# PSUM banks handed out by age, the scores of two heads in turn, and VectorE making the whole low half outside the experts

## The reference, cut to what matters

```python
logits = jnp.einsum('bhnid,bhnjd->bhnij', qb, kb) * SCALE
lo = jnp.where(ii[:, None] >= ii[None, :], lo + own_bias[None, :, None], NEG)
```

## Time and profile before

| | |
|---|---|
| median of three executions | 1948.52 us |
| profiled execution, its time | 1950.66 us |
| span of its instructions | 1948.9 us |
| TensorE matmul busy | 1788.9 us, 92% |
| VectorE busy | 1224.6 us, 63% |
| ScalarE busy | 968.1 us, 50% |
| GpSimd busy | 927.0 us, 48% |
| granted TensorE clock, mean | 0.944 |
| ScalarE's high half of a unit, mean | 1912 ns |
| HBM read | 336.76 MB |

### The profile page before, as it was taken

How to read it: one execution, slowest core, us unless ns; L and a number is a source line. 1 busy time by engine, 2 the same in 40 slices (tenths; PEclk the granted TensorE clock), 3 DMA queues, 4 the chain that set the end, 5 groups by cost and what they waited for, 6 DMA issues and landing times.

```text
span 1948.9 us, 30590 instructions
## 1 busy us (share of the span) xinstructions
PE 1788.9 (92%) x12222; PEld 1649.9 (85%) x12222; DVE 1224.6 (63%) x1841; ACT 968.1 (50%) x1406; POOL 927.0 (48%) x525
## 2 busy tenths in 40 slices
PE   6999999998899998989979999899878999999996
PEld 5988899987789998978879999778767878888875
DVE  4656554455554545866764444877767878787783
ACT  3455554345545533444435433444426767676762
POOL 5431566543136655312245446312243777786860
PEclk8999999999879999989989999889878999999996
DMA  6522345552224555322325445423325888888980
GB/s 242 195 89 101 127 172 178 195 195 87 87 88 165 181 176 205 131 86 84 112 87 173 173 176 172 164 88 108 109 87 194 316 309 323 299 324 308 340 307 24
DMA packets 50019, 339.95 MB, mean 174 GB/s; under 512 B 5511, under 2 KB 7775, under 8 KB 10031
## 3 DMA queue, kind: packets, MB, share of 16 engines
q1 hardware_dynamic: 47152, 328.79, 46.3%
q0 software_dynamic: 2720, 9.13, 1.5%
HBM read 336.76 MB, written 1.13 MB: 173 GB/s over the span
## 4 chain that ended last, share of the span: by engine, by line
PE 66%; DVE 17%; ACT 6%; issue 5%; POOL 3%; DMA 0%; DVEq 0%; SPq 0%; ACTq 0%; POOLq 0%
PE bank L408 11%; PE bank L410 11%; PE bank L409 11%; DVE CA L1657 5%; PE bank L786 4%; PE bank L787 4%; PE bank L788 4%; ACT wh L975 3%; DVE wl L1381 3%; POOL wl L1972 2%; PE bank L544 2%; PE bank L817 2%; PE bank L545 2%; PE bank L486 2%; PE bank L546 2%
## 5 line engine op out<-in xcount | busy, mean ns | idle before, releaser
L1972 POOL TENSOR_TENSOR wl<-stg,wh 128x512 fp32r<-128x512 f32 x311 | 784.6, 2529 | 856.1 <-ACT wh L975 855.4
L1381 DVE TENSOR_TENSOR wl<-stg,wh 128x1536 fp32r<-128x1536 f32 x311 | 592.6, 1911 | 343.0 <-ACT wh L975 342.6
L975 ACT ACTIVATE wh<-stg 128x2048 fp32r<-128x2048 f32 x311 | 594.2, 1912 | 231.2 <-PE bank L410 114.6
L408 PE MATMUL bank<-xh,wh 128*128 128x256 f32 (+1 forms) x1472 | 431.5, 293 | 10.0 <-POOL wl L1972 4.8
L410 PE MATMUL bank<-xh,wl 128*128 128x256 f32 (+1 forms) x1472 | 424.9, 289 | 0.0
L409 PE MATMUL bank<-xl,wh 128*128 128x256 f32 (+1 forms) x1472 | 424.4, 288 | 0.0
L408 PEld LDWEIGHTS bank<-xh,wh 128*128 128x128 f32 x1472 | 284.0, 193 | 13.9 <-issue 11.6
L409 PEld LDWEIGHTS bank<-xl,wh 128*128 128x128 f32 x1472 | 283.5, 193 | 0.7
L410 PEld LDWEIGHTS bank<-xh,wl 128*128 128x128 f32 x1472 | 283.9, 193 | 0.0
L544 PE MATMUL bank<-wh,xh 128*128 128x256 f32 x480 | 144.5, 301 | 33.9 <-DVE xl L1420 17.3
L786 PE MATMUL bank<-wh,GH 128*128 128x512 f32 (+3 forms) x400 | 148.0, 370 | 0.1
(11 more groups left out here) (256 smaller groups left out, 3211.5 us busy)
## 6 DMA issues: line engine op xcount, KB each, us to landing
stg<-in_w SPq DMA_DIRECT2D x311, 1024.0 KB, 4.8
BT<-bias_scratch POOLq DMA_DIRECT2D x3, 1024.0 KB, 11.4
BT<-bias_scratch POOLq DMA_DIRECT2D x1, 2048.0 KB, 12.2
BB<-bias_scratch POOLq DMA_DIRECT2D x2, 1024.0 KB, 8.2
res<-in_x SPq DMA_DIRECT2D x1, 1024.0 KB, 5.7
BB<-bias_scratch POOLq DMA_DIRECT2D x2, 512.0 KB, 8.6
out<-res SPq DMA_DIRECT2D x1, 1024.0 KB, 4.6
consts<-in_consts SPq DMA_DIRECT2D x1, 320.0 KB, 5.7
```

Source lines behind the costliest of these rows:

```text
L408: pe.matmul(out, wh, xh(kt), start=kt == 0, stop=False)
L975: act.activation(WH[u % NW][:, :], stg[u % NS][:, :], ACT.Copy).then_inc(*m.inc("w_high", u))
L1381: vec.tensor_tensor(WL[u % NW][:, 0:VW], stg[u % NS][:, 0:VW], WH[u % NW][:, 0:VW].bitcast(F32), ALU.subtract).then_inc(*m.inc("w_low_v", u))
L1972: pool.tensor_tensor(WL[u % NW][:, VW:], stg[u % NS][:, VW:], WH[u % NW][:, VW:].bitcast(F32), ALU.subtract).then_inc(*m.inc("w_low_g", u))
```

## The change

Three parts, all in one diff.

1. `bank` keeps a list `line` of the banks and gives the first one that is not held, moving it to the end; `let_go` moves banks that were held to the end of the list when they are released.
2. The jobs come in the order (head h, tt 0), (h+1, tt 0), (h, tt 1), (h+1, tt 1), and `scores` does nothing for odd i; for even i it issues the scores of jobs i and i+1, one matmul of each in turn. Their banks are taken together, for each group of segments one bank of each job.
3. For units under `MOE_UNIT` VectorE subtracts all 2048 columns and GpSimd none; the waits for GpSimd's part go for these units on TensorE and on the DMA queue. The experts keep the split at 1536.

```diff
-                    for hh in range(4 * hq, 4 * hq + 4):
+                    for h0, tt, hh in ((h0, tt, h0 + j) for h0 in (4 * hq, 4 * hq + 2) for tt in range(2) for j in range(2)):
...
-            turn, held, frees = [0], set(), [()] * 8
+            line, held, frees = list(range(8)), set(), [()] * 8
...
-                while turn[0] % 8 in held:
-                    turn[0] += 1
-                b = turn[0] % 8
-                turn[0] += 1
+                b = [i for i in line if i not in held][0]
+                line.remove(b)
+                line.append(b)
...
+            def let_go(*banks):
+                for b in banks:
+                    held.discard(b)
+                    line.remove(b)
+                    line.append(b)
...
-                w.wait_ge(*m.of("w_low_g", u))
+                if u >= MOE_UNIT:
+                    w.wait_ge(*m.of("w_low_g", u))
...
             def scores(l, i):
+                if i % 2:
+                    return
+                two = JOBS1[l][0][i:i + 2]
...
-                    b, old = bank(("score", l, i, s0), ("biased", (l, i, s0)))
-                    vacant(old)
+                    bs = [bank(("score", l, i + k, s0), ("biased", (l, i + k, s0))) for k in range(2)]
+                    for b, old in bs:
+                        vacant(old)
                     for n in range(s0, s1):
...
+                        for k in range(2):
+                            lhs, rhs = two[k]["segs"][n]
+                            ins = pe.matmul(PS[bs[k][0]][:, (n - s0) * wd:(n - s0 + 1) * wd], lhs, rhs, start=True, stop=True)
...
-                        held.clear()
+                        let_go(*sorted(held))
...
             def split(u):
                 w.wait_ge(*m.of("w_high", u))
-                vec.tensor_tensor(WL[u % NW][:, 0:VW], stg[u % NS][:, 0:VW], WH[u % NW][:, 0:VW].bitcast(F32),
+                n = VW if u >= MOE_UNIT else UT * P
+                vec.tensor_tensor(WL[u % NW][:, 0:n], stg[u % NS][:, 0:n], WH[u % NW][:, 0:n].bitcast(F32),
                                   ALU.subtract).then_inc(*m.inc("w_low_v", u))
...
             def split(u):
+                if u < MOE_UNIT:
+                    return
                 w.wait_ge(*m.of("w_high", u))
                 pool.tensor_tensor(WL[u % NW][:, VW:], stg[u % NS][:, VW:], WH[u % NW][:, VW:].bitcast(F32),
...
-                    w.wait_ge(*m.of("w_low_g", u - NS))
+                    if u - NS >= MOE_UNIT:
+                        w.wait_ge(*m.of("w_low_g", u - NS))
```

More of the change, by code:

```diff
@@ L282, in mixer_jobs @@
                 if l == 1 or g == 2:
-                    for hh in range(4 * hq, 4 * hq + 4):
+                    for h0, tt, hh in ((h0, tt, h0 + j) for h0 in (4 * hq, 4 * hq + 2) for tt in range(2) for j in range(2)):
                         lst = [(g3, hh) for g3 in range(3)] if l == 0 else [(hh // 8, hh % 8)]
[L285 to L295, removed]
+                        nk = P * (tt + 1)
+                        segs, chunks = [], []
+                        for si, (g3, h) in enumerate(lst):
+                            po, pr = 64 * (h % 2), g3 * 4 + h // 2
+                            segs.append((QT[po:po + 64, 0, pr, tt * P:(tt + 1) * P], QT[po:po + 64, 1, pr, 0:nk]))
+                            for k in range(tt + 1):
+                                chunks.append((si * nk + k * P, P, VT[:, k, g3, h * 64:(h + 1) * 64]))
+                        bias = BT.rearrange("p (g h) s -> p g h s", h=8)[:, lst[0][0]:lst[-1][0] + 1, lst[0][1], S - nk:S]
+                        jobs.append(dict(nq=P, nk=nk * len(lst), segs=segs, add=bias, chunks=chunks, gi=gi,
+                                         out=O[:, tt, hh * 64:(hh + 1) * 64]))
                 due[gi] = len(jobs)
@@ L450, in scores @@
             def scores(l, i):
[L451 to L455, removed]
+                if i % 2:
+                    return
+                two = JOBS1[l][0][i:i + 2]
+                nb = two[0]["add"].shape[1]
+                wd = two[0]["nk"] // nb
+                w.wait_ge(*m.of("turned", (l, "last", two[0]["gi"])))
                 for s0 in range(0, nb, 512 // wd):
                     s1 = min(nb, s0 + 512 // wd)
-                    b, old = bank(("score", l, i, s0), ("biased", (l, i, s0)))
-                    vacant(old)
+                    bs = [bank(("score", l, i + k, s0), ("biased", (l, i + k, s0))) for k in range(2)]
+                    for b, old in bs:
+                        vacant(old)
                     for n in range(s0, s1):
-                        lhs, rhs = j["segs"][n]
-                        ins = pe.matmul(PS[b][:, (n - s0) * wd:(n - s0 + 1) * wd], lhs, rhs, start=True, stop=True)
-                    ins.then_inc(*m.inc("group", ("score", l, i, s0)))
+                        for k in range(2):
+                            lhs, rhs = two[k]["segs"][n]
+                            ins = pe.matmul(PS[bs[k][0]][:, (n - s0) * wd:(n - s0 + 1) * wd], lhs, rhs, start=True, stop=True)
+                            if n == s1 - 1:
+                                ins.then_inc(*m.inc("group", ("score", l, i + k, s0)))
             def turn_over(tag, a, i, j):
@@ L606, in feature_sum @@
                     ins.then_inc(*m.inc("group", (name, "mean")))
-                    held.discard(sums[name])
+                    let_go(sums[name])
             def shift_sum(stage, name):
@@ L923, in tensor_program @@
             few = w.eng.value_load(CNI[0:1, 0:1])
-            state = (turn[0], list(frees), at[0], dict(w.seen))
+            state = (list(line), list(frees), at[0], dict(w.seen))
             with w.eng.If(few <= P):
@@ L927, in tensor_program @@
                 w.eng.drain().then_inc(*m.inc("joined_pe", "few"))
-            turn[0], frees[:], at[0], w.seen = state[0], state[1], state[2], dict(state[3])
+            line[:], frees[:], at[0], w.seen = state[0], state[1], state[2], dict(state[3])
             with w.eng.Else():
@@ L2109, in gpsimd_program @@
             sp.at, sp.made, w.seen = state[0], state[1], dict(state[2])
-            m.count["w_low_g"] = sp.made
+            m.count["w_low_g"] = sp.made - MOE_UNIT
             with w.eng.Else():
```

## The result

The changed kernel takes 1903.34 us in the median of four executions (1898.54 to 1905.48), the kernel before, run beside it, 1948.6: a ratio of 0.9759, 95% interval 0.9736 to 0.9783, some 46 us faster. The profiled execution spans 1900.6 us, 48.3 us less than before.

A forecast was written before the change was run, and what follows sets the result against it. TensorE, busy 92% of the span, was taken as the bound, with gains only at its waits and half-clock stretches. 12 + 3.8 + 2.5 + 4 + 1.7 + 8.8 + 1.4 = 34.2 us gave 1914, range 1901 to 1938.

The forecast's parts named there:

- Banks by age: Mixers: TensorE's eight 2 us waits for a bank's copy go; 12 us gained in mixer 1's rounds, 3.8 in mixer 0.
- Scores in pairs: Mixers: 24 fewer score blocks at 0.30 us and half the possible row-half overlap; 4 us in the tails, rest counted elsewhere.
- first rival: Mixers: VectorE and ScalarE chains keep what the banks give, all but half-clock stretches; 15 us less gain, 1929; chance 0.15.
- VectorE's whole low half: Scaled q and k waits 2.5 us, TensorE's waits for GpSimd 1.7, mix layers 8.8, start and mix-layer ends 1.4.
- The waits of rows 2 and 3 shrunk by 9 us: Mix layers, sign of being right: TensorE's 15.5 us of waits for chains through VectorE shrink by 9 us.
- Direct waits for the low half: Three places where TensorE waits for GpSimd's part, 4.8 us in all: unit ready 0.56 us sooner, 1.7 us gained.
- line 408 [...] for the low half: Sign of being wrong: TensorE at line 408 or 544 waiting for the low half; no size given.
- Start and ends: Program start and ends of the mix layers, where GpSimd's sums stand behind its low half: 1.4 us gained.
- Costs at nothing: Feed-forward blocks and dense layer: VectorE's longer low half (+0.54 us a unit) is hidden, so no gain or loss.
- Slower: Mixers: a pair's second score bank waits for VectorE's whole turn, 16 pairs, 46 us lost, 1960; chance 0.04.
- The addition not paid back: Mix layers give 0 and not 8.8 us if something besides GpSimd's low half holds taps up: 1923; chance 0.08.
- 25 to 45: Whole kernel: the main forecast's band of time lost, in us; chance 0.66.

The follow-up runs named there:

- e3: Kernel before with only VectorE's whole low half for units below 179: 1923.4 us, ratio 0.9889.
- e10: Changed kernel with transposes three steps behind the scores, not two, in mixer 1 and the mix layers: 1909.7 us, ratio 0.9802.
- e6: Changed kernel with GpSimd subtracting as many scratch columns per unit as before in the mix layers, and waiting for high halves below unit 179: 1931.0 us, ratio 0.9915.
- e9: Changed kernel with job order and scores as before, so banks by age and whole low half only: 1904.5 us, ratio 0.9772.
- e1: Kernel before with only the banks given out by age: 1932.3 us, ratio 0.9921.
- e11: Changed kernel without score pairs and with transposes three steps behind the scores in mixer 1 and the mix layers: 1904.5 us, ratio 0.9762.
- e4: Changed kernel with the first head's score matmuls of each block all issued before the second head's: 1904.9 us, ratio 0.977.

## Why the prediction was right, and where its sum was not

- **Banks by age (12 + 3.8).** Right in mechanism and, alone, in size: 15 us for 16 expected, with 6.1 us of waits that came back in mixer 1 for 5.9 in the sum's terms. Mixer 0 is 8.0 us shorter with all parts (the sum's share for it, with one of its tails, was about 7) and mixer 1 13.4. The waits came back where the forecast put them, lines 487 and 536, but up to 1.9 us and not 1.2, and 12.6 us in all at line 487 with the pairs in place.
- **Scores in pairs (4 in the tails, some 4 in the rounds).** This step failed twice, in opposite ways. On TensorE the saving was larger than taken: the overlap of row halves is full, not half, and for the narrow matmuls too. In time it can't be told from zero beside the other parts. The sum took the tails as bound by TensorE; but in the changed kernel they wait for exponentials as well (2.7 us in mixer 0's), and the lower clock behind them takes 1.5 us more. The first rival's mechanism, chains that keep what is given, holds for the pairs and not for the banks.
- **VectorE's whole low half (2.5 + 1.7 + 8.8 + 1.4).** Right in mechanism, 14.4 us taken and some 22 measured alone. The mis-sized term is the mix layers: 8.8 forecast, 17.4 by stage in e3 (7.4 + 7.0 + 3.8 - 0.7). VectorE's own balance in the first two stretches came out at 13.0 us and not 8.8. The taps gave what was taken (12.9 and 12.0 us), but mix layer 0's low halves, 1.83 us in the mean before, grew by 6.9 us and not 8.1, and the first operation of each tap chain, held up like the taps (four in each layer; in mix layer 1 they took 1.02 us each before and 0.42 in e3), was not counted: 2.8 us in both layers. The stretch behind mix layer 1's convolution (3.8, of it 2.3 by the clock) stood in no term. Nor did the stage behind mixer 1: its projection and first feed-forward gemm, 1008 matmuls in both kernels, took 4.5 us less. The waits there are the same, 2.4 us before and 2.1 after; before, the granted clock was low behind one of 1.5 us (0.69 from 575 to 586 us), and after it was not behind one of 1.7 us. No run shows why. "The waits of rows 2 and 3 shrunk by 9 us" did not come: they shrank by 4.4, although the layers gave twice the forecast.
- **Direct waits for the low half.** 4.8 us of the earlier trace rows became 2.1 for line 1394 and 1.4 for line 987: 1.3 us, for 1.7 taken. The forecast's sign of being wrong, "line 408 [...] for the low half", thus did appear, with less than half of the wait of before. **Start and ends (1.4):** the first matmul came 0.6 us later, not earlier, and the wait for GpSimd's sums at the ends went from 8.4 to 8.3 us. This term gave nothing.
- **Costs at nothing.** The second gemms of both feed-forward blocks took the same time (89.61 and 101.54 us), and so did, to 0.5 us, the stretch from mix layer 0's output gemm to mix layer 1, with the dense SwiGLU in it. The 0.54 us per unit is hidden there. GpSimd's squares between the gemms rose from 614 to 1384 ns in the mean: 32 of the 64 now run while VectorE's low half does and take 2.15 us, the other 32 take 0.61 as before. They are hidden too.
- **The rivals.** "Slower" did not occur (0.8 us for the second score bank), but e10 shows its mechanism at 10.6 us once the lag is three. "The addition not paid back" is refuted by e3, and e6 shows that it was GpSimd's operation that held the taps up.
- **Range and chances.** The gain, 45 us by the medians and 47 by the ratio, lies at the upper edge of the "25 to 45" that had a chance of 0.66. By stage the mixers gave 21.4 us for the 22.3 taken (12 + 3.8 + 2.5 + 4), and that is in part luck: the pairs, some 8 of it, gave 1.9 there, and the banks and the low half gave the other 19.6 (e9). The mix layers and the stage behind mixer 1 gave some 13 us more than taken. The range's low end is a slip, 1914 - 4 - 8 is 1902 and not 1901, and so is "1.05 us per 1024 columns": 1.758 - 0.682 is 1.08, and half of that is the 0.54 that the sum uses.
- **What stays open.** Banks and low half alone add to 37 us by their ratios (15 + 22), and together they give 44 (e9), each with an error of 3 to 5 us. Whether they help each other can't be said: in the profiles they do not, where e1 and e3 are 22 and 33 us shorter and e9 46. Nor is it shown why the mix layers of e11 are slower, and which wait sets the clock behind mixer 1.

## What to carry to other kernels

Before counting what an engine saves, ask which chain it will meet next: TensorE was freed of 17 us of scores, 9 of them in mixer 1, and waited for exponentials instead; the kernel without pairs (e9) is as fast. Where two engines disturb each other, giving all of the work to the one that is already the busier can win: here its other instructions are short and many, 120 taps of 0.5 us in each mix layer. And read from a trace which engine sets the length of a stretch before crediting TensorE's clock with a gain: where VectorE did, 2.5 us less of busy TensorE changed nothing, and where TensorE did, behind mixer 0's tail, a clock of 0.76 instead of 1.00 cost 1.5 us.

## What was not expected of the hardware

Score matmuls of 64 rows on different row halves run fully side by side: twelve in 1.57 us, six in 1.56 before. The Trainium skill (TensorEngine Tiling, Key Properties) says that different tiles can work in parallel; the rows now agree. They do so out of program order: in e4 the second head's first matmul starts 14 ns after the first head's first, with three records of the first head between them in the program.

A stage without waits repeats exactly: the first feed-forward block's second gemm took 89.61 us in all fourteen kernels, while whole executions of one kernel differ by 3 to 14 us.
